# Two pieces of TensorE work change places: the last recurrence level in the first block, and a pair of transposes in the forgetting attention

## The chip, the core and the metric

One core of a Trainium2 chip runs the whole program. The metric is the device time of one execution in microseconds; the time before is the median of three runs. The engines have names in the profile: PE is TensorE's products, PEld its weight loads, DVE VectorE, ACT ScalarE, POOL GpSimd, and SP the queue that issues most of the loads.

## The reference, cut to what matters

A sequence of 256 tokens of width 1024 passes through four mixers. The first block has two layers, each with a gated recurrence (HGRN2) beside sparse attention; the second has an LRU layer and a layer with spatial gating beside forgetting attention, each with a feed-forward network. All of it is float32. The parts that the change touches:

```python
# first block, both layers: the recurrence and its gates
o_hg = hgrn2_chunkwise(heads(hq, HG_HEADS), log_f, k_hg, heads(hi, HG_HEADS))
o_hg = rmsnorm(o_hg, hgrn_onorm_g[i]).transpose(0, 2, 1, 3).reshape(B, T, HG_W)
y_hg = o_hg * jax.nn.sigmoid(hgo) * jax.nn.silu(hz)
...
kc = rmsnorm(compress(heads(kcm, KVH), cmp_pe[i, 0], cmp_w1[i, 0], cmp_w2[i, 0]), nsa_knorm_g[i, 0])
...
# second block, second layer: forgetting attention
logits = (jnp.einsum('bhqd,bhkd->bhqk', qb, k).astype(jnp.float32) * scale
          + cb[..., None] - c[:, :, None, :])
logits = jnp.where(key_pos[None, :] <= q_pos[:, None], logits, -jnp.inf)
p = jax.nn.softmax(logits, axis=-1)
return jnp.einsum('bhqk,bhkd->bhqd', p.astype(v.dtype), v)
```

## The kernel before, in words

**Products in three passes.** Every large product is written as three float32r products of rounded parts (`product3`, L477 to L481: low weight by high input, high by low, high by high). So each weight panel of 128 by 2048 is split before use: ScalarE casts the raw panel to the high part (`high_part`, L1374, the row L1381), VectorE subtracts to get the low part (`low_part`, L2006, the row L2009). There are three slots each for the raw panel, the high part and the low part. A cast waits until the panel three earlier in the row has been used up; the product waits for the low part (`split`, L465).

**An order written out by hand.** Each engine runs its own list of instructions, in order. TensorE's list is written first, and where it has issued a piece of work it notes a step with `todo(...)` in an agenda, with a place number that says how many accumulations were closed by then. ScalarE's and VectorE's lists walk this agenda and emit their share of every step in the same order; after a step they may also emit panel casts (`split_high`, L1385) and low parts (`split_low`, L2014) that the place number allows. So where a step stands in the agenda decides what stands ahead of it on two other engines.

**PSUM.** There are eight banks. `begin(name, b)` (L424) makes TensorE wait until whatever last filled bank b has been read out; `done` (L433) tells the readers that it is full. `drained` makes an engine wait for the read-out.

**The first block, around the change (both layers, L803 to L861).** The recurrence is built in eight levels, 0 to 7, each in two groups g. A level's products go to bank 7 for g = 0 and to bank 0 for g = 1 (L769); VectorE copies them out and then updates query and key (`level`, L2243), which frees the bank with the copy and lets the next level's products start with the last update (L2284, waited for in L768). `some(2)` issues one level. The gate panels hgo, hz and nz are cut into chunks of 24 products (`gate_chunk`, L787), two for each panel. The first panel, hgo0, goes to bank 6, every later one to bank 0 (L793); ScalarE copies hgo0 out in the step `copy`. Before the change the order on TensorE is: the product for the compressed hidden layer (L842), the first chunk of hgo0, level 7, the steps `k_norm` and `q_norm`, the second chunk of hgo0, the two products kc and vc (L855 and L856), the first chunk of hgo1, and so on. On VectorE the steps come as hidden (L2339), level 7, then k_norm, which begins with the low part of the panel hz0 (L2327).

**The forgetting attention (L1191 to L1214).** `tokens` (L543) multiplies by the value panels fv0 and fv1: for each half of the rows (h = 0, 1) it runs both token tiles (n = 0 into bank 0, n = 1 into bank 1). Between the two halves stands `first_value_half` (L1183), which ends in `turned(0)`: six transposes of probabilities (`turn`, L689) into banks 6 and 7. Before the change `turned(1)` follows when both tiles of the second half are done. Then come the first products of the output (L1163, into bank 0), `weigh(0)` and `weigh(1)` (probabilities by values, L709 and L711), `turned(2)`, more output products and `turned(3)`. `turned(u)` waits for the probabilities that the step `normalise u` on VectorE makes (L2047); this in turn needs the exponentials that ScalarE emits with the step `turned u-2` (L1794 to L1797). ScalarE's step `fv` (L1807) copies the two value tiles out of banks 0 and 1, and the step `fo 0` on VectorE (L2625) copies the first weighted values out.

Of the kernel before, what the change touches and what calls it, by code (L numbers as in the profile page):

```python
# [14 lines left out]
HALF = 512  # L15
# [140 lines left out]
LOADS, LOAD_NO, SPLIT_NO = panel_plan()  # L156
# [7 lines left out]
def build(nc, a, out):  # L164
# [4 lines left out]
    with ExitStack() as ctx:  # L169
# [156 lines left out]
        for name, rows in VEC_ROWS:  # L326
# [5 lines left out]
            while done_rows < rows:  # L332
                at = VEC_AT[name] + done_rows
                n = min(rows - done_rows, P - at % P)
# [86 lines left out]
        def _(pe):  # L421
            last_done = [None]

            def begin(name, b):  # L424

                k = bank_fills[b]
                bank_fills[b] += 1
                fills[name] = (b, k)
                if k > 0:
                    pe.wait_ge(psum_free[b], k)  # L430
                return ps[b]

            def done(name, ins):  # L433

                order_of[name] = len(order_of)
                ins.then_inc(psum_full[fills[name][0]], 1)
                last_done[0] = name
# [102 lines left out]
                    else:  # L540
                        ins.then_inc(psum_full[b[i]], 1)

            def tokens(names, b, keys, cols=HALF, between=None, normed=False):  # L543

                for n in range(NT):
                    begin(names[n], b + n)
                for h, key in enumerate(keys):
                    split(key)
                    if normed:
                        pe.wait_ge(xn_ready, NKH * (h + 1))  # L550
                    for n in range(NT):
                        ins = by_token(ps[b + n][:, 0:cols], parts(key, NKH, cols), n, h)
                        if h == 1:
                            done(names[n], ins)
                    if h == 0:
                        ins.then_inc(half_done, 1)
                        halves[0] += 1
                        freed(key, (half_done, halves[0]), len(order_of) - 1)
                        if between:
                            between()  # L560
                release(keys[1])
# [34 lines left out]
            for h in range(2):  # L596
                pe.wait_ge(x_landed[h], 16)
                for g in (2 * h, 2 * h + 1):
                    b = (0, 3, 4, 7)[g]
                    begin(f"x{g}", b)  # L600
                    for j in range(4):
                        c, n = 2 * g + j // 2, j % 2
# [136 lines left out]
            for l in range(DEPTH):  # L739
                todo = noting(l)  # L740
# [46 lines left out]
                def gate_chunk():  # L787

                    if not gate_chunks:
                        return  # L790
                    name, g, j = gate_chunks.pop(0)
                    key = (f"{name}{g}", l)
                    b = 6 if key[0] == "hgo0" else 0  # L793
                    if j == 0:
                        begin(f"{name}{g}_{l}", b)
                        split(key)
                    ins = chunk(ps[b][:, j * T:(j + 1) * T], parts(key), j * P)
                    if j == 1:
                        done(f"{name}{g}_{l}", ins)
                        release(key)  # L800
                        todo(("copy", f"{name}{g}"))
# [3 lines left out]
                def some(k):  # L805
                    for _ in range(min(k, len(levels))):
                        level(*levels.pop(0))
# [36 lines left out]
                done(f"hid_{l}", ins)  # L844
                todo(("hidden",))
                gate_chunk()
                some(2)
                todo(("k_norm",))
                todo(("q_norm",))


                gate_chunk()
                pe.wait_ge(w2_landed, 48 * (l + 1))
                pe.wait_ge(hidden_ready, l + 1)
                product(f"kc_{l}", 5, 32, W2[:, 0:P], HID[:, 0:32])  # L855
# [105 lines left out]
                def turned(u):  # L961
                    turn(f"n{l}", u, pidx + u)
                    todo(("turned", u))
# [67 lines left out]
                for g in range(4):  # L1031
                    b = (7, 6, 1, 2)[g]
# [14 lines left out]
            for l in range(DEPTH):  # L1047
                L = DEPTH + l
                todo = noting(L)
# [22 lines left out]
                else:  # L1072
# [119 lines left out]

                    pair_scores(0)
                    todo(("normalise", 0))
                    tokens(["fv0", "fv1"], 0, [("fv0", L), ("fv1", L)], between=first_value_half)
                    todo(("fv",))
                    turned(1)
                    todo(("normalise", 2))
                    output_rows(0, range(0, 4))
                    weigh(0)  # L1200
                    weigh(1)
# [155 lines left out]
        def _(act):  # L1357
# [27 lines left out]
            def split_high(place, most=len(SPLIT_KEYS)):  # L1385

                while next_high[0] < most:
                    q = next_high[0]
                    key = SPLIT_KEYS[q]
                    if q >= SLOTS and split_from.get(q, 1 << 30) > place or len(key) == 3 and \  # L1390
                            key not in (("gate", key[1], 0), ("value", key[1], 0)):
                        break
                    n = LOAD_NO[key]
                    high_part(n, q % SLOTS, panel_size(n), panel_free[SPLIT_KEYS[q - SLOTS]] if q >= SLOTS else None)
                    high_from[q] = place
                    next_high[0] += 1
# [102 lines left out]
            tile, r, n, c0, c1, src = gain_dma  # L1499
            act.dma_start(vrows[r:r + n, tile, c0:c1], src).then_inc(gain_rows_landed, 16)  # L1500
            turned = {}
# [27 lines left out]
            for g in range((NVT + 3) // 4):  # L1529
                s, n = 16 if g == 0 else 0, min(512, NVEC - 512 * g)  # L1530
# [172 lines left out]
            for l in range(DEPTH):  # L1703
# [61 lines left out]
                else:  # L1765
# [23 lines left out]
                    for place, step, *arg in agenda[DEPTH + l]:  # L1789
                        if step == "scores":  # L1790
                            if arg[0] == 0:
                                for k in range(2):
                                    exps_of_kind("f", 0, k, 8)
                        elif step == "turned":  # L1794
                            turned_copies("f", arg[0], pidx + arg[0])
                            if arg[0] < 2:
                                exps_of_kind("f", 1, arg[0], 8 + 1)  # L1797
                        elif step == "sg1":
                            mixed_high(DEPTH + l, None, (0, 1))
                        elif step == "zg":  # L1800
                            for n in range(NT):
                                full(act, f"zg{n}")
                                f(QN[:, n * 512:(n + 1) * 512], bank(f"zg{n}")[:, :],
                                  ACT.Gelu_apprx_tanh).then_inc(free(f"zg{n}"), 1)
                            drained(act, "zg1")
                            f(NZ[:, :], QN[:, :], ACT.Square).then_inc(act_part, 1)
                        elif step == "fv":  # L1807
                            copy_out("fv0", vh[:, 0, :], bank("fv0")[:, :])
                            copy_out("fv1", vh[:, 1, :], bank("fv1")[:, :])
                        elif step == "fo":  # L1810
                            mixed_high(DEPTH + l, ["fo0", "fo1"], (2 + arg[0],))
                        elif step == "zg_norm":
                            log_exp()
                            act.wait_ge(dve_part, 4)
                            link(f(NT16[:, :], NT16[:, :], ACT.Ln, bias=EPSC[:, 0:1], scale=1.0 / 64))
                            f(NT16[:, :], NT16[:, :], ACT.Exp, scale=-0.5).then_inc(act_part, 1)
                        elif step == "zu":
                            g = arg[0]
                            full(act, f"zu{g}")
                            f(SG[:, g * 512:(g + 1) * 512], bank(f"zu{g}")[:, :],  # L1820
                              ACT.Gelu_apprx_tanh).then_inc(free(f"zu{g}"), 1)
                        split_high(place)


                def output_drained(g):
# [115 lines left out]
        def _(dve):  # L1941
# [72 lines left out]
            def split_low(place, most=len(SPLIT_KEYS)):  # L2014

                while next_low[0] < most and next_low[0] in high_from and high_from[next_low[0]] <= place:
                    q = next_low[0]
                    n = LOAD_NO[SPLIT_KEYS[q]]
                    low_part(n, q % SLOTS, q + 1, panel_size(n))
                    next_low[0] += 1  # L2020
# [202 lines left out]
            for l in range(DEPTH):  # L2223
# [66 lines left out]
                for place, kind, *arg in agenda[l]:  # L2290
# [33 lines left out]
                                                  const(tab).unsqueeze(1).to_broadcast([P, 4, T]), ALU.mult)  # L2324
                        ins.then_inc(rope_ready, 1)
                    elif kind == "k_norm":
                        split_low(place, SPLIT_NO[("hz0", l)] + 1)  # L2327
                        dve.wait_ge(k_rinv_ready, l + 1)
                        for j in range(2):
                            s = slice(j * T, (j + 1) * T)  # L2330
# [8 lines left out]
                    elif kind == "hidden":  # L2339
# [8 lines left out]
                        V.tensor_copy(HIDV[:, :].rearrange("p (g r c) -> p g r c", g=2, r=4),  # L2348
                                      HID[:, 32:64].rearrange("p (g c) -> p g c", g=2).unsqueeze(2)
                                      .to_broadcast([P, 2, 4, 16])).then_inc(hidden_ready, 1)  # L2350
                    elif kind == "cmp_kv":
                        full(dve, f"vc_{l}")
                        V.tensor_tensor(v3(VCB, 8), const("head16").unsqueeze(2).to_broadcast([P, 8, 64]),
# [106 lines left out]
            for l in range(DEPTH):  # L2460
# [77 lines left out]
                else:  # L2538
# [4 lines left out]
                    for name in ("fq0", "fq1", "fk0", "fk1"):  # L2543
# [3 lines left out]
                        if name == "fq1":  # L2547
                            n = LOAD_NO[("ff", DEPTH + l)]
# [29 lines left out]
                    in_first = False  # L2578
                    for place, kind, *arg in agenda[DEPTH + l]:
# [50 lines left out]
                            mixed_low(DEPTH + l, 2 + g)  # L2630
                        if (kind, *arg) != ("turned", 0):
                            in_first = (kind, *arg) == ("zu", 1) or in_first and (kind, *arg) != ("scores", 1)
                        if not in_first:
                            split_low(place)
                nidx += 1
                if l == 0:
# [113 lines left out]
            for n in range(NT):  # L2750
                b = fills[f"res{n}0"][0]
# [159 lines left out]
```

## Time and profile before

| what | us |
|---|---|
| median of three runs | 976.4 (976.29 to 976.43) |
| the profiled execution, its own time | 976.13 |
| its span from first to last instruction | 974.1 |
| TensorE's products busy | 956.4 (98% of the span) |
| TensorE's weight loads busy | 876.3 (90%) |
| VectorE busy | 753.9 (77%) |
| ScalarE busy | 615.9 (63%) |
| mean granted TensorE clock | 0.999 of full speed |

The 2.0 us between the span and the profiled execution's time lie around the program. Spans of products overlap, since they are pipelined, so the distance between the starts of two products is what one costs. A row of the timeline gives start, duration, engine, line, operation, out<-in, the sizes and the count; idle time of the engine ahead of it stands in brackets with what ended it.

### The profile page before, as it was taken

The numbers are of one execution on the slowest core, as the hardware profiler recorded it, in microseconds if no ns is written. First come the engines' busy times: TensorE is split into PE (matmuls) and PEld (weight loads), VectorE is DVE, ScalarE is ACT, GpSimd is POOL, SyncE is SP. The second block draws the span as 40 slices with busy tenths as digits, with TensorE's granted clock in tenths as the row PEclk, the third lists the DMA queues.
The fourth block names the chain that finished last, engine by engine and source line by source line (L and its number), as shares of the span: only waits on it lengthen the run. The fifth ranks groups of instructions, "written<-read, shape, count | busy, mean of one in ns | idle before, by whom it ended". The sixth has DMA issues, their size and how long they took to land.

```text
span 974.1 us, 18775 instructions
## 1 busy us (share of the span) xinstructions
PE 956.4 (98%) x7618; PEld 876.3 (90%) x7618; DVE 753.9 (77%) x1132; ACT 615.9 (63%) x914; POOL 19.7 (2%) x33
## 2 busy tenths in 40 slices
PE   7999999999999999999999999999999999999997
PEld 6998989998989889999999999999898988888886
DVE  7967876787578767898788877778777598777685
ACT  5745885676447856787477556567657567555554
POOL 2000200000002000000000000000000000000000
PEclk9999999999999999999999999999999999999999
DMA  9666422465664233745546655557283446555541
GB/s 307 194 177 218 139 88 87 154 194 189 167 217 138 74 101 124 233 156 190 174 132 214 217 176 203 181 177 221 89 265 109 134 143 218 198 189 173 190 154 44
DMA packets 143870, 164.33 MB, mean 169 GB/s; under 512 B 6687, under 2 KB 130217, under 8 KB 143801
## 3 DMA queue, kind: packets, MB, share of 16 engines
q1 hardware_dynamic: 142408, 161.90, 51.5%
q0 software_dynamic: 928, 0.52, 0.4%
q8 instruction: 51, 0.84, 0.4%
q10 hardware_dynamic: 464, 0.93, 0.2%
q14 instruction: 19, 0.15, 0.0%
HBM read 161.89 MB, written 1.05 MB: 167 GB/s over the span
## 4 chain that ended last, share of the span: by engine, by line
PE 86%; DVE 7%; ACT 3%; issue 2%; DMA 1%; SPq 0%; DVEq 0%; ACTq 0%
PE ps L479 18%; PE ps L480 18%; PE ps L481 18%; PE ps L1247 14%; PE ps L1245 7%; DVE panels_low L2009 2%; ACT panels_high L1381 2%; DVE squares L1972 1%; PE ps L497 1%; PE ps L684 1%; DVE input_parts L1968 1%; DMA panels<-in_w_in 1%; PE ps L780 1%; PE ps L709 1%; PE ps L1287 1%
## 5 line engine op out<-in xcount | busy, mean ns | idle before, releaser
L2009 DVE TENSOR_TENSOR panels_low<-panels,panels_high 128x2048 fp32r<-128x2048 f32 (+1 forms) x145 | 327.5, 2261 | 67.4 <-ACT panels_high L1381 67.2
L1381 ACT CAST panels_high<-panels 128x2048 fp32r<-128x2048 f32 (+1 forms) x145 | 273.4, 1887 | 83.7 <-PE ps L481 62.2
L479 PE MATMUL ps<-input_parts,panels_low 128*128 128x256 f32 x832 | 241.5, 290 | 1.5 <-DVE panels_low L2009 0.8
L480 PE MATMUL ps<-input_parts,panels_high 128*128 128x256 f32 x832 | 235.2, 283 | 0.0
L481 PE MATMUL ps<-input_parts,panels_high 128*128 128x256 f32 x832 | 235.1, 283 | 0.0
L1247 PE MATMUL ps<-input_parts,panels_high 128*128 128x512 f32 x608 | 213.7, 395 | 0.0
L1245 PE MATMUL ps<-input_parts,panels_low 128*128 128x256 f32 x608 | 170.6, 281 | 0.7 <-DVE panels_low L2009 0.7
L479 PEld LDWEIGHTS ps<-input_parts,panels_low 128*128 128x128 f32 x832 | 159.0, 191 | 6.1 <-issue 2.6
L480 PEld LDWEIGHTS ps<-input_parts,panels_high 128*128 128x128 f32 x832 | 159.2, 191 | 0.6 <-issue 0.5
L481 PEld LDWEIGHTS ps<-input_parts,panels_high 128*128 128x128 f32 x832 | 159.2, 191 | 0.0
L1247 PEld LDWEIGHTS ps<-input_parts,panels_high 128*128 128x128 f32 x608 | 114.1, 188 | 26.1
L1245 PEld LDWEIGHTS ps<-input_parts,panels_low 128*128 128x128 f32 x608 | 114.7, 189 | 2.5 <-issue 1.3
L479 PE MATMUL ps<-ffn_hidden_high,panels_low 128*128 128x256 f32 x320 | 91.4, 286 | 0.2 <-DVE panels_low L2009 0.2
L481 PE MATMUL ps<-ffn_hidden_high,panels_high 128*128 128x256 f32 x320 | 90.7, 283 | 0.0
L480 PE MATMUL ps<-ffn_hidden_low,panels_high 128*128 128x256 f32 x288 | 81.2, 282 | 0.0
L479 PEld LDWEIGHTS ps<-ffn_hidden_high,panels_low 128*128 128x128 f32 x320 | 61.0, 191 | 1.1 <-DVE panels_low L2009 0.4
L481 PEld LDWEIGHTS ps<-ffn_hidden_high,panels_high 128*128 128x128 f32 x320 | 60.4, 189 | 0.0
L480 PEld LDWEIGHTS ps<-ffn_hidden_low,panels_high 128*128 128x128 f32 x288 | 54.3, 188 | 0.3
L1906 ACT CAST ffn_hidden_high<-values_hg 128x512 fp32r<-128x512 f32 x22 | 13.7, 621 | 57.1 <-DVE values_hg L2686 53.7
L1875 ACT COPY forget_key<-ps 128x512 f32<-128x512 f32 x36 | 21.0, 583 | 44.2 <-PE ps L1247 44.2
L479 PE MATMUL ps<-unscaled,panels_low 128*128 128x256 f32 x160 | 46.2, 289 | 0.0
L481 PE MATMUL ps<-unscaled,panels_high 128*128 128x256 f32 x160 | 45.2, 283 | 0.0
(342 smaller groups left out, 1626.7 us busy)
## 6 DMA issues: line engine op xcount, KB each, us to landing
panels<-in_ffn_up SPq DMA_DIRECT2D x44, 1024.0 KB, 5.1
panels<-in_w_in SPq DMA_DIRECT2D x29, 1024.0 KB, 5.8
panels<-in_ffn_down SPq DMA_DIRECT2D x22, 1024.0 KB, 4.9
panels<-in_mix_w_in SPq DMA_DIRECT2D x20, 1024.0 KB, 5.5
panels<-in_w_out SPq DMA_DIRECT2D x8, 1024.0 KB, 5.2
panels<-in_w_pg SPq DMA_DIRECT2D x8, 1024.0 KB, 5.0
panels<-in_mix_w_out SPq DMA_DIRECT2D x8, 1024.0 KB, 5.2
panels<-in_w_in SPq DMA_DIRECT2D x6, 512.0 KB, 5.7
```

The source lines that it names most:

```text
L479: pe.matmul(dst, w[1], x[0], start=start, stop=False if not kw else True, **kw)
L480: pe.matmul(dst, w[0], x[1], start=False, stop=False if not kw else True, **kw)
L481: return pe.matmul(dst, w[0], x[0], start=False, stop=stop, **kw)
L497: ins = pe.matmul(dst, w3[:, k, col:col + m], x3[:, k, :], start=(k == 0), stop=(k == nk - 1))
L684: ins = pe.matmul(ps[b + r][:, 0:2 * w].rearrange("p (k s) -> p k s", k=2), q[h, n * P:(n + 1) * P], keys[h, :, r, 0:w], start=False, stop ...
L709: pe.matmul(o[64 * r:64 * r + 64, :], vals(0, r), pt_lo[bb][:, r, :], start=start, stop=True, skip_group_check=True)
L1245: pe.matmul(both[:, 0, :], w_low, xh3[:, k, :], start=(k == 0), stop=True, skip_group_check=True)
L1247: ins = pe.matmul(both, w_high, x_parts[:, :, k, :], start=False, stop=True, skip_group_check=True)
L1381: nc.scalar.copy(high_slots[slot][:, 0:size], raw[n % SLOTS][:, 0:size]).then_inc(high_ready, 1)
L1875: nc.scalar.copy(sums[par][:, s, :], up_halves[half][:, :, 0, :]).then_inc(half_out, 1)
L1906: nc.scalar.copy(gh3[par], hidden[par]).then_inc(gh_ready, 1)
L2009: V.tensor_tensor(low_slots[slot][:, 0:size], raw[n % SLOTS][:, 0:size], high_slots[slot][:, 0:size].bitcast(F32), ALU.subtract).then_inc( ...
```

## The change

Three places move, and no arithmetic changes. In the first block the second chunk of hgo0 goes ahead of level 7, so that the products of level 7 stand behind two gate chunks in place of one; the steps k_norm and q_norm stay behind level 7. With this, VectorE's low part of hz0 moves from the head of the step k_norm to the end of the step hidden, which is ahead of level 7. In the forgetting attention `turned(1)` and the step `normalise 2` move from behind the second value half to a place between its two token tiles, and no panel is split at the step `turned 1`.

```diff
-            def tokens(names, b, keys, cols=HALF, between=None, normed=False):
+            def tokens(names, b, keys, cols=HALF, between=None, normed=False, amid=None):
...
                         if h == 1:
                             done(names[n], ins)
+                            if n == 0 and amid:
+                                amid()
...
                 todo(("hidden",))
                 gate_chunk()
+                gate_chunk()
                 some(2)
                 todo(("k_norm",))
                 todo(("q_norm",))
-
-
-                gate_chunk()
                 pe.wait_ge(w2_landed, 48 * (l + 1))
...
                     todo(("normalise", 0))
-                    tokens(["fv0", "fv1"], 0, [("fv0", L), ("fv1", L)], between=first_value_half)
+                    def second_value_half():
+
+                        turned(1)
+                        todo(("normalise", 2))
+
+                    tokens(["fv0", "fv1"], 0, [("fv0", L), ("fv1", L)], between=first_value_half,
+                           amid=second_value_half)
                     todo(("fv",))
-                    turned(1)
-                    todo(("normalise", 2))
                     output_rows(0, range(0, 4))
...
-                        split_high(place)
+                        if (step, *arg) != ("turned", 1):
+                            split_high(place)
...
                     elif kind == "k_norm":
-                        split_low(place, SPLIT_NO[("hz0", l)] + 1)
                         dve.wait_ge(k_rinv_ready, l + 1)
...
                                       .to_broadcast([P, 2, 4, 16])).then_inc(hidden_ready, 1)
+                        split_low(place, SPLIT_NO[("hz0", l)] + 1)
                     elif kind == "cmp_kv":
...
-                        if not in_first:
+                        if not in_first and (kind, *arg) != ("turned", 1):
                             split_low(place)
```

## Rows read from the trace of the kernel before

**Rows 1.** The page: busy time of each engine, share of the span, instructions.

```profile
PE 956.4 (98%) x7618; PEld 876.3 (90%) x7618; DVE 753.9 (77%) x1132; ACT 615.9 (63%) x914; POOL 19.7 (2%) x33
```

**Rows 2.** What TensorE waited for: total us, times, longest us.

```profile
PE ps L780 <- DVE forget_key L2284: 1.5, 2, 0.8
PE ps L695 <- DVE probs L2063: 1.1, 1, 1.1
```

**Rows 3.** Timeline of TensorE, first layer: level 7, chunk, kc, hgo1's first product.

```profile
91.08 0.68 PE L780 MATMUL ps<-query,forget_key 128*64 128x64 f32 x8
92.47 0.68 PE L780 MATMUL ps<-query,forget_key 128*64 128x64 f32 x8 [0.71 <-DVE forget_key L2284]
93.08 0.38 PE L479 MATMUL ps<-input_parts,panels_low 128*128 128x256 f32 x1
...
96.06 0.31 PE L589 MATMUL ps<-cmp_hidden,cmp_w 128*128 128x32 f32 x2
...
96.42 0.36 PE L479 MATMUL ps<-input_parts,panels_low 128*128 128x256 f32 x1
```

**Rows 4.** Timeline of VectorE, first layer: level 7's two copies, hz0's low part.

```profile
93.54 0.41 DVE L2264 COPY decay_diag<-ps 64x256 f32<-64x256 f32 x1
...
94.54 0.41 DVE L2264 COPY decay_diag<-ps 64x256 f32<-64x256 f32 x1
...
95.55 2.28 DVE L2009 TENSOR_TENSOR panels_low<-panels,panels_high 128x2048 fp32r<-128x2048 f32 x1
```

**Rows 5.** Timeline of ScalarE, first layer: hz0's cast, the end of the norms.

```profile
88.36 1.90 ACT L1381 CAST panels_high<-panels 128x2048 fp32r<-128x2048 f32 x1
...
92.69 1.06 ACT L1367 ACTIVATE gate_z<-gate_z 128x1024 f32<-128x1024 f32 x1
```

**Rows 6.** Timeline elsewhere: a low part, and the first product that waited for it.

```profile
225.60 2.29 DVE L2009 TENSOR_TENSOR panels_low<-panels,panels_high 128x2048 fp32r<-128x2048 f32 x1 [0.19 <-ACT panels_high L1381]
...
228.04 0.35 PE L479 MATMUL ps<-input_parts,panels_low 128*128 128x256 f32 x1 [0.28 <-DVE panels_low L2009]
```

**Rows 7.** Timeline of TensorE, forgetting attention: tile 1, turned(1), output, turned(2), turned(3).

```profile
746.22 0.39 PE L479 MATMUL ps<-panels_high,input_parts 128*128 128x512 f32 x1
...
748.95 0.27 PE L695 MATMUL ps<-consts,probs 128*128 128x128 f32 x1
...
749.52 0.36 PE L479 MATMUL ps<-ffn_hidden_high,panels_low 128*128 128x256 f32 x1
...
755.27 0.33 PE L695 MATMUL ps<-consts,probs 128*128 128x128 f32 x1 [1.13 <-DVE probs L2063]
...
758.85 0.27 PE L695 MATMUL ps<-consts,probs 128*128 128x128 f32 x1
```

**Rows 8.** Timeline of ScalarE in the same stretch.

```profile
745.29 0.47 ACT L1367 ACTIVATE probs<-ps,neg_max 128x256 f32<-128x256 f32 x1 [0.36 <-DVE neg_max L2043]
...
746.89 0.60 ACT L1372 COPY values_hg<-ps 128x512 f32<-128x512 f32 x1
...
751.43 0.86 ACT L1372 COPY probs_t<-ps 128x512 f32<-128x512 f32 x2
752.17 0.50 ACT L1367 ACTIVATE probs<-ps,neg_max 128x256 f32<-128x256 f32 x1
```

**Rows 9.** Timeline of VectorE in the same stretch.

```profile
746.38 4.49 DVE L2009 TENSOR_TENSOR panels_low<-panels,panels_high 128x2048 fp32r<-128x2048 f32 x2
751.57 2.29 DVE L2009 TENSOR_TENSOR panels_low<-panels,panels_high 128x2048 fp32r<-128x2048 f32 x1 [0.71 <-ACT panels_high L1381]
753.78 0.16 DVE L2056 TENSOR_SCALAR prob_sums<-prob_sums 128x4 f32<-128x4 f32 x1
...
755.13 0.68 DVE L2628 COPY squares<-ps 128x512 f32<-128x512 f32 x1
...
757.52 1.03 DVE L2063 TENSOR_TENSOR probs<-probs,prob_sums 128x256 f32<-128x256 f32 x2
```

**Rows 10.** A stretch: us, busy PE, PEld, DVE, ACT, POOL, then PEclk, DMA.

```profile
755.30:760.00 4.70, 4.70 (x41) 4.70 (x42) 2.49 (x6) 1.89 (x5) 0.00 (x0) 1.00 0.88 281
```

## The prediction

> **What bounds the kernel now.** I read the page's busy times first, then the list of TensorE's waits, then the timelines around the places that the change touches. TensorE's products are busy for 98% of the span, VectorE 77% [rows 1]. So an edit is worth only what it does to TensorE's few gaps. The list of waits names two that lie at these places: 1.5 us in two waits, one for each layer of the first block, where the products of level 7 (L780) wait for level 6's last update (L2284), and one of 1.1 us, where turned(2) (L695) waits for its probabilities (L2063) [rows 2]. Nothing else on the list lies there, and TensorE's later waits come at the end of chains that its own products start, so time won or lost here goes through to the end.
>
> **Level 7 behind the second chunk: the wait that goes.** Level 7's two groups start at 91.08 and 92.47, and the next chunk at 93.08 [rows 3]. The second group ran without a stop and took 0.61 to the next product, so both need 1.22 of the 2.00 that they took: 0.78 us were lost. Behind a second chunk, 2.98 us long (93.08 to 96.06), level 6 has been done for long, and this loss goes. hgo1's first product, at 96.42 before, would be wanted at 95.64.
>
> **What is late next.** That product opens bank 0, and bank 0 was last filled by the second group of level 7. So it waits until VectorE has copied that group out. Before, VectorE did this at 94.54, long before the bank was wanted [rows 4]. In the new order the low part of hz0 stands ahead of level 7 on VectorE. Its cast has ended at 90.26 [rows 5], so nothing holds it back: it starts at 93.54, where level 7's first copy started before [rows 4]. From the start of a low part to the next instruction go 2.21 us (751.57 to 753.78) [rows 9], so level 7's first copy comes at 95.75, the second 1.00 later, as before, and it ends 0.41 after that, at 97.16 [rows 4]. From the end of such a release to TensorE's first product go 0.15 us (227.89 to 228.04) [rows 6]. hgo1 starts at 97.31, not at 95.64: a new stop of 1.67 us takes the place of 0.78, and the layer loses 97.31 - 96.42 = 0.89 us. Two layers with the same pattern (waits of 0.7 and 0.8 [rows 2]): **+1.78 us**.
>
> The bounds for a layer are -0.78, where bank 0 would not hold TensorE at all, and +0.89, where it holds as worked out. I take the upper, as each step of it is an order in the program with a duration from a row. VectorE's sum of work is the same, so it reaches k_norm when it did.
>
> On ScalarE hgo0's copy now stands ahead of both norms and waits for the second chunk, which ends near 94.06 (95.64 less 0.36 for kc and vc, less 1.22). The copy takes 0.60 (the like copy of [rows 8]), and the norms 3.5 (90.26 to 93.75 [rows 5]), so they are out at about 98.2, well behind the 93.75 of before. VectorE takes up k_norm at 97.75 as before (its work is the same, in another order) and q_norm after that; k's inverse comes ahead of q's on ScalarE, so both are met, and POOL's additions, which follow these two steps, start when they did. The next thing that TensorE wants from ScalarE, the squares of kc, it wants behind hgo1's chunk, at 97.31 + 2.98 = 100.29. Some 2 us of cover: I price it at nothing. Without the stop at bank 0 TensorE would be there at 98.62 and this cover would be about gone. No load is issued by a moved step on any queue. The slot of hz0's raw panel comes free 2 us sooner, which only helps.
>
> A rule speaks for a smaller loss. [Rows 6] show 0.15 us between a release and the first product. The Trainium skill, TensorE: Matmul & The Clock Gate, section "Architectural detail: the array is 16× 32×32, not 1× 128×128", says that TensorE's queue can pull weight loads ahead of products in flight; if that hid the load behind each of the three new stops, the sum would be, as an estimate by that page, 0.45 us smaller. The row differs, and I keep it.
>
> **turned(1) between the tiles.** Tile 1 of the second half takes 2.73 us (746.22 to 748.95), the six transposes 0.57 (to 749.52) [rows 7]. They change places, so the output's first product is still wanted at 749.52. The gain lies at turned(2). Before, normalise 2 stood on VectorE behind the low part of a panel whose cast came late: 751.57, then 753.78 [rows 9]. Now the step comes ahead of that panel: the two low parts before it end at 750.87, normalise 2 takes 1.35 (753.78 to 755.13) [rows 9], and its result is there at 752.2. The wait of 1.13 goes.
>
> But the output's first product opens bank 0, which holds value tile 0, and ScalarE's copy of that tile now comes behind the copies and the exponentials of turned 1. ScalarE is free at 746.89, as the transposes end; the copies take 0.74 (751.43 to 752.17), the four exponentials 1.60 (745.29 to 746.89), so the tile's copy runs from 749.23 to 749.83 [rows 8]. With 0.15 [rows 6] TensorE starts at 749.98, 0.46 late. turned(2) follows 4.62 later (755.27 - 1.13 - 749.52) [rows 7], at 754.60, against 755.27: **-0.67 us**.
>
> Does turned(3) hold? It is wanted 3.58 later (755.27 to 758.85) [rows 7], at 758.18. Its probabilities come 3.42 after the start of the copy of the first weighted values (755.13 to 758.55) [rows 9], which follows the weighing, at 754.6, if VectorE is free. The late panel: tile 1's copy ends near 750.4, the cast takes 1.90 (as in [rows 5]), the low part 2.21, so VectorE is free at 754.5. Ready at 758.0 to 758.1: it just holds, with 0.1 to spare. If the stop at bank 0 were shorter, turned(3) would wait instead, so this part moves little. Bounds: -1.13, if nothing waits, and +0.64 (rival three).
>
> **The sum.** +1.78 - 0.67 = +1.11 us. The profiled execution took 976.13 and would take 977.24; the median of the runs lies 0.27 above it, and I put the same shift on it: **977.5 us**. A measurement of this kernel tells about 0.2% (1.95 us) from no change, so this is "no change", on the slow side of it.
>
> **The rivals.**
> One, faster: bank 0 does not hold TensorE in the first block. For it: the wait that is removed is plain in the list. Against it: the line that picks the bank (L793) and VectorE's 2.2 us panel. Then 2 x -0.78 - 0.67 = -2.23: 974.2. Chance 10%.
> Two: the low part of hz0 comes behind level 7 after all, since the place number does not yet allow it. TensorE starts level 7 at 94.06, its first group ends at 94.74, the second copy is out 1.41 later, at 96.15, hgo1 starts at 96.30: -0.12 for a layer, in all -0.91: 975.5. Chance 8%. This would also be the change not doing what it says.
> Three, slower: in the forgetting attention the late panel still stands ahead of normalise 2 on VectorE. It decides if ScalarE may cast that panel at an earlier step than the tiles' copies. Then its low part ends at 754.5, normalise 2 at 755.85, and turned(2) starts near 755.9, 0.64 later than before: 1.78 + 0.64 = +2.42: 978.8. Against it: the panel's slot comes free only with tile 1. Chance 8%.
> Four, slower: the granted clock falls in the new stop of 1.67 us. After the stop of 1.13 the clock was 1.00, the 2.4 GHz level [rows 10]; a stop of 1.67 within running work the trace does not have. At half the clock one chunk more of 2.98 us would be lost in each layer: some 983.5. [...] The rows show no fall. Chance 3%.
>
> **How the numbers follow.** The forecast has 66% and its own range 976.6 to 978.3, rival two 8%, and 5% is left for what I have not seen. 975.2 to 978.9 takes in the forecast, two and three, and leaves out one, four and the rest. Faster by over 0.2% (under 974.45) is rival one: 0.10. Slower by over 0.2% (over 978.35) is three, four and the forecast's edge: 0.12. Within: 0.78.
>
> **What would show it.** Right: L780 no longer in the list of TensorE's waits; in its place two waits of about 1.6 us of a product L479 for VectorE's copy L2264; one of about 0.4 for ScalarE's copy L1372; no wait at turned(2). On VectorE the low part stands ahead of L2264. Wrong: hgo1's chunk without a wait ahead of it (rival one), L2264 ahead of the low part (two), a wait of L695 for L2063 that is still there (three), PEclk under 1.00 after a stop (four).

## The result and the profile after

| what | us |
|---|---|
| before, median of 22 executions | 976.34 |
| after, median of 22 executions | 977.59 |
| ratio, 95% interval | 1.0018, 1.0012 to 1.0024 |
| the profiled execution of after, its span | 977.38, 975.3 |

The change costs 1.25 us by the medians, which is 0.13% and under the 0.2% (1.95 us) that the prediction takes as what a measurement can tell from no change; the interval of the ratio lies just clear of 1. 977.5 had been forecast. One execution of each kernel lies far off (1882.31 and 5295.99 us); the medians hardly feel it. Behind the changed places the lines of the kernel are a few higher: L780 is now L782, L695 is L697, L1372 is L1376, L2009 is L2014, L2056 is L2061, L2264 is L2269.

What TensorE waits for in the kernel after (total us, times, longest; the DMA waits are the start of the program):

```profile
PE ps L597 <- DMA q_nope<-in_norm_g: 5.6, 1, 5.6
PE ps L479 <- DVE decay_diag L2269: 3.1, 2, 1.5
PE ps L605 <- DMA forget_key<-in_x: 1.2, 1, 1.2
PE ps L479 <- DVE panels_low L2014: 0.8, 3, 0.3
PE ps L1249 <- DVE panels_low L2014: 0.8, 2, 0.4
```

Both entries of [rows 2] are gone. In the place of level 7's wait in each layer stands another, twice as long: a gate chunk's product (L479) waits until VectorE has copied level 7 out (L2269).

TensorE after, first layer: level 7, kc and vc, hgo1's first product. To be compared with [rows 3].

```profile
94.09 1.15 PE L782 MATMUL ps<-query,forget_key 128*64 128x64 f32 x16
95.17 0.41 PE L591 MATMUL ps<-cmp_hidden,cmp_w 128*128 128x32 f32 x2
95.41 0.41 PE L591 MATMUL ps<-cmp_w,cmp_hidden_rep 128*128 128x64 f32 x2
97.35 0.39 PE L479 MATMUL ps<-input_parts,panels_low 128*128 128x256 f32 x1 [1.52 <-DVE decay_diag L2269]
```

Level 7's 16 products now run in one piece, and TensorE stands still for 1.52 us behind kc and vc, ahead of hgo1. The reason is on VectorE, to be compared with [rows 4]:

```profile
93.69 2.28 DVE L2014 TENSOR_TENSOR panels_low<-panels,panels_high 128x2048 fp32r<-128x2048 f32 x1
95.89 0.41 DVE L2269 COPY decay_diag<-ps 64x256 f32<-64x256 f32 x1
...
96.89 0.41 DVE L2269 COPY decay_diag<-ps 64x256 f32<-64x256 f32 x1
```

The low part of hz0 stands ahead of the two copies; the second copy ends at 97.30 and TensorE goes on at 97.35. All that lies ahead of the changed place already comes 0.15 us later than before (hgo0's first product at 88.18, before at 88.03), so this product is 97.35 - 96.42 - 0.15 = 0.78 us late, and about as much in the second layer (a stop of 1.53).

TensorE after, forgetting attention (against [rows 7]): turned(1), tile 1, the output's first product, turned(2), turned(3).

```profile
748.00 0.27 PE L697 MATMUL ps<-consts,probs 128*128 128x128 f32 x1
...
748.57 0.48 PE L479 MATMUL ps<-panels_high,input_parts 128*128 128x512 f32 x1
...
751.68 0.38 PE L479 MATMUL ps<-ffn_hidden_high,panels_low 128*128 128x256 f32 x1
...
756.25 0.33 PE L697 MATMUL ps<-consts,probs 128*128 128x128 f32 x1
...
759.84 0.33 PE L697 MATMUL ps<-consts,probs 128*128 128x128 f32 x1
```

This stretch begins 1.77 us later than before (the second half's first product at 745.14, before at 743.37). turned(2) comes 756.25 - 755.27 = 0.98 later: 0.79 were won. The output's first product is 751.68 - 749.52 - 1.77 = 0.39 late, since its bank waits for ScalarE. The list of TensorE's waits above doesn't name this stop; the row of the product's weight load does:

```profile
751.68 0.19 PEld L479 LDWEIGHTS ps<-ffn_hidden_high,panels_low 128*128 128x128 f32 x1 [0.54 <-ACT values_hg L1376]
```

VectorE of after in the same stretch, normalise 2 and the late panel (against [rows 9]):

```profile
752.55 0.16 DVE L2061 TENSOR_SCALAR prob_sums<-prob_sums 128x4 f32<-128x4 f32 x1
...
754.03 2.29 DVE L2014 TENSOR_TENSOR panels_low<-panels,panels_high 128x2048 fp32r<-128x2048 f32 x1
```

normalise 2 (from 752.55) is now ahead of the late panel's low part (754.03), behind which it stood before. ScalarE of after, turned 1's copies and the copies of the two value tiles (against [rows 8]):

```profile
748.66 0.87 ACT L1376 COPY probs_t<-ps 128x512 f32<-128x512 f32 x2
...
750.99 1.21 ACT L1376 COPY values_hg<-ps 128x512 f32<-128x512 f32 x2
```

The value tiles come at 750.99, behind turned 1's copies and its exponentials; the first of the two copies ends near 751.6, and the output's first product starts at 751.68. By the trace the changed places sum to 2 x 0.78 - 0.79 = +0.77. The two profiled executions differ by more, by 1.25 us: 0.15 of it is there before the first changed place, 0.06 comes between the layers, and about 0.25 behind the last changed place, between 759 and 821 us, where a second profile of the same kernel (e11, below) has 0.05. In e11 the two stops are 1.59 and 1.65 us and the changed places sum to +0.96, so one profile's +0.77 is good to some 0.2. The twelve shortest executions (976.89 to 977.60, middle 977.2, all at a mean granted clock of 0.999) lie 0.85 above the median before, and 0.95 above the middle of the twelve shortest before (976.2). The rest of the median's +1.25 comes from longer executions, of which more below.

### The profile page after: what moved, and what is told of

Same layout as the page of the kernel before. It is cut to its first block, busy times and chain, and to the rows that moved or that the text cites. A ratio compares the mean times of both kernels' runs of the same rounds, so it can differ in the third digit from the quotient of the medians.

```text
span 975.3 us, 18775 instructions
## 1 busy us (share of the span) xinstructions
PE 957.3 (98%) x7618; PEld 877.0 (90%) x7618; DVE 754.1 (77%) x1132; ACT 615.9 (63%) x914; POOL 19.8 (2%) x33
## 4 chain that ended last, share of the span: by engine, by line
PE 86%; DVE 8%; ACT 3%; issue 2%; DMA 1%; SPq 0%; DVEq 0%; ACTq 0%
PE ps L479 18%; PE ps L480 18%; PE ps L481 18%; PE ps L1251 14%; PE ps L1249 7%; DVE panels_low L2014 2%; ACT panels_high L1385 2%; DVE squares L1977 1%; PE ps L497 1%; PE ps L686 1%; DVE input_parts L1973 1%; PE ps L711 1%; PE ps L782 1%; DMA forget_key<-in_x 1%; PE ps L1291 1%
## 5 line engine op out<-in xcount | busy, mean ns | idle before, releaser
L2014 DVE TENSOR_TENSOR panels_low<-panels,panels_high 128x2048 fp32r<-128x2048 f32 (+1 forms) x145 | 327.5, 2261 | 67.5 <-ACT panels_high L1385 67.4
L479 PE MATMUL ps<-input_parts,panels_low 128*128 128x256 f32 x832 | 241.3, 290 | 4.5 <-DVE decay_diag L2269 3.1
L479 PEld LDWEIGHTS ps<-input_parts,panels_low 128*128 128x128 f32 x832 | 159.2, 191 | 9.3 <-DVE decay_diag L2269 3.3
L479 PE MATMUL ps<-ffn_hidden_high,panels_low 128*128 128x256 f32 x320 | 91.7, 287 | 0.1
L479 PEld LDWEIGHTS ps<-ffn_hidden_high,panels_low 128*128 128x128 f32 x320 | 61.4, 192 | 1.0 <-ACT values_hg L1376 0.5
L479 PE MATMUL ps<-unscaled,panels_low 128*128 128x256 f32 x160 | 46.2, 289 | 0.0
```

What stands on the lines that cost most here:

```text
L479: pe.matmul(dst, w[1], x[0], start=start, stop=False if not kw else True, **kw)
L2014: V.tensor_tensor(low_slots[slot][:, 0:size], raw[n % SLOTS][:, 0:size], high_slots[slot][:, 0:size].bitcast(F32), ALU.subtract).then_inc( ...
```

## The experiments

Theory: the loss is level 7's late read-out, because VectorE does hz0's low part first; the gain is normalise 2 ahead of the late panel. Rivals: TensorE's new order costs time by itself, or what is late is ScalarE's norms (no wait of the list above names them).

**One part of the change at a time.** e1 has the first block's edit alone, e2 that of the forgetting attention alone.

e1, against the kernel before:

```diff
                 gate_chunk()
+                gate_chunk()
                 some(2)
                 todo(("k_norm",))
                 todo(("q_norm",))
-                gate_chunk()
...
                     elif kind == "k_norm":
-                        split_low(place, SPLIT_NO[("hz0", l)] + 1)
...
                                       .to_broadcast([P, 2, 4, 16])).then_inc(hidden_ready, 1)
+                        split_low(place, SPLIT_NO[("hz0", l)] + 1)
```

> The kernel before with the first block's edit alone (second gate chunk ahead of level 7, hz0's low part ahead of level 7 on VectorE); the forgetting attention as before. My theory: hgo1's first product stops for bank 0 in both layers, about 1.5 us each, while the waits of 0.71 and 0.76 at level 7 are gone; net +0.8 us a layer, so about +1.6 us against the kernel before. Its executions should also lie as wide apart as those of the whole change if these stops are what spreads them (some with a mean granted clock under 0.999). Rival: the loss of the whole change comes from the forgetting attention or from the two parts together; then this one is at -1.5 to 0 us.

e2, against the kernel before (with the conditions on `("turned", 1)` of the change):

```diff
...
-                    tokens(["fv0", "fv1"], 0, [("fv0", L), ("fv1", L)], between=first_value_half)
+                    def second_value_half():
+
+                        turned(1)
+                        todo(("normalise", 2))
+
+                    tokens(["fv0", "fv1"], 0, [("fv0", L), ("fv1", L)], between=first_value_half,
+                           amid=second_value_half)
                     todo(("fv",))
-                    turned(1)
-                    todo(("normalise", 2))
```

> The forgetting attention's edit alone; the first block as before. My theory: the wait of 1.13 us at turned(2) is gone, the output's first product starts some 0.4 us later for bank 0, net -0.8 us. Executions as close together as those of the kernel before. Rival: this part costs time too (0 to +0.6 us), or is worth the whole 1.13 us.

e2 took 975.57 against 976.33, ratio 0.9991 (0.9982 to 1.0): -0.76, as the trace of the whole had it (0.79), though the interval reaches 1. e1's two shortest executions took 977.84 and 977.85, +1.5, which is the theory's loss (2 x 0.78); its median was 979.25, ratio 1.0031 (1.0019 to 1.0044), since four executions took 979.2 to 981.0 with a mean granted clock of 0.995 to 0.997. TensorE's waits in the profiled execution of e1 (977.85):

```profile
PE ps L479 <- DVE decay_diag L2262: 3.1, 2, 1.6
PE ps L695 <- DVE probs L2061: 1.1, 1, 1.1
```

The parts are independent: the first block's stop is there without the second edit, and the wait at turned(2) is there without it too. 1.52 less 0.76 is 0.76; the trace of the whole has 0.77.

**The low part back behind level 7** (e3), and, the other way round, **the low part alone moved** (e5: the kernel before with VectorE's move and nothing else).

e3, against the kernel after:

```diff
                     elif kind == "k_norm":
+                        split_low(place, SPLIT_NO[("hz0", l)] + 1)
...
                                       .to_broadcast([P, 2, 4, 16])).then_inc(hidden_ready, 1)
-                        split_low(place, SPLIT_NO[("hz0", l)] + 1)
```

> The whole change, but hz0's low part back at the head of the step k_norm, behind level 7 on VectorE. My theory: the place of this low part is the whole of the loss. VectorE copies level 7's first group when its products end, about 94.8, the second group is out at about 96.2, and hgo1's first product starts near 96.35 instead of 97.35: 1.0 us a layer better than the whole change, -0.2 a layer against the kernel before, so with -0.8 from the forgetting attention about -1.1 us in all. A stop for bank 0 of about 0.5 us stays in each layer. Rival: the second chunk ahead of level 7 is what costs, wherever the low part stands: +0.5 to +1.2 us as for the whole change.

e5, against the kernel before:

```diff
                     elif kind == "k_norm":
-                        split_low(place, SPLIT_NO[("hz0", l)] + 1)
...
                                       .to_broadcast([P, 2, 4, 16])).then_inc(hidden_ready, 1)
+                        split_low(place, SPLIT_NO[("hz0", l)] + 1)
```

> The kernel before with one edit alone: hz0's low part ahead of level 7 on VectorE. TensorE's order is as before, so the wait of 0.7 us at level 7 stays. My theory: bank 0 is freed at 97.2 as in the whole change, so hgo1's first product, wanted at 96.45, stops for about 0.8 us: +0.8 to +0.9 us a layer, +1.7 us in all, as much as the first part's edit costs in its fastest executions (977.84 against 976.33). The two stops of 0.7 and 0.8 us stand apart. If the executions of the first part lie wide apart (977.84 to 980.97, mean granted clock down to 0.995) because one stop of 1.5 us makes the clock fall in some of them, these here lie close together, near 978.0. Rival: whatever holds TensorE up in this stretch spreads them, and these do too; or the low part's move alone costs little (under +0.6 us), and the second chunk ahead of level 7 is needed for the loss.

e3 took 975.00, 0.9986 (0.9977 to 0.9995): -1.33 where the change has +1.25, so putting one VectorE instruction back turns the sign. TensorE's stop in the first layer of e3, by the timeline:

```profile
96.45 0.38 PE L479 MATMUL ps<-input_parts,panels_low 128*128 128x256 f32 x1 [0.46 <-DVE decay_diag L2269]
```

e5 took 978.01 against 976.41, 1.0017 (1.0008 to 1.0026): +1.60, the same loss as e1's with TensorE's order of before. Level 7's wait stays, and a second stop joins it, as TensorE's timeline of e5 shows:

```profile
93.05 0.68 PE L780 MATMUL ps<-query,forget_key 128*64 128x64 f32 x8 [0.72 <-DVE forget_key L2284]
...
97.80 0.39 PE L479 MATMUL ps<-input_parts,panels_low 128*128 128x256 f32 x1 [0.60 <-DVE decay_diag L2264]
```

So the whole loss of the first block is VectorE's move, and TensorE's new order by itself is a gain. The rival of a costly order is out. The 0.46 us left in e3 say that even with the low part behind, level 7's two copies are late for a bank that is wanted right behind kc and vc.

**Another bank for hgo1** (e4, against the kernel after), so that it needs no read-out of level 7.

```diff
-                    b = 6 if key[0] == "hgo0" else 0
+                    b = {"hgo0": 6, "hgo1": 4}.get(key[0], 0)
```

> The whole change, but hgo1's chunks go to bank 4 in place of bank 0. Bank 4's last content, the sums of the key squares, is read by ScalarE's first norm at about 95.4. My theory: bank 0 is what holds TensorE, so the stop of 1.5 us goes and hgo1 starts at about 95.75; the squares of kc are then wanted at 98.7, just when ScalarE has them (98.6), so at most 0.1 us is lost there. 1.5 us a layer better than the whole change: about -2.3 us against the kernel before. Rival: TensorE stops elsewhere for the same late VectorE work (at kc's squares or at the cross product, which waits for level 7's update), and less than half of this comes back: -0.8 us or worse.

It took 974.94, 0.9984 (0.9975 to 0.9994): -1.39, and 0.9 less was gained than expected. The stop at hgo1 is gone, as the theory has it. But the time did not all go through. TensorE's timeline of e4, further on in the first layer:

```profile
103.13 0.46 PE L883 MATMUL ps<-decay_diag,values_hg 128*128 128x128 f32 x2 [0.18 <-issue]
```

The recurrence's output products come some 0.35 us late in each layer. With TensorE 1.7 us ahead (hgo1 at 95.66), ScalarE is what is late: its cast of hz1 (98.55, 1.89 us) stands ahead of the copies that these products read. The squares of kc, which stand behind the norms on ScalarE, are late too, by less: they start 3.04 us behind hgo1's first product (98.70 - 95.66), before it was 2.96 (99.38 - 96.42), and the cross product follows them after 0.24 in place of 0.14, in all 0.18 us.

**That cast behind the step `cross`** (e6: e4 and this).

```diff
-                    if not parts_out and (not in_units or step == "turned" and arg[0] % 2 == 1):
+                    if step not in ("cmp_kv", "kc_norm", "spread") and not parts_out and (
+                            not in_units or step == "turned" and arg[0] % 2 == 1):
```

> The whole change with hgo1 in bank 4 (the run before, -1.39 us), and on ScalarE the cast of hz1 moved from the step cmp_kv to the step cross, behind the copies of the decay blocks and of the cross product. In the bank 4 run the recurrence's output products start at 103.13, 0.35 us after the chunk ahead of them allows, and ScalarE works without a gap from 94 on with that cast in the middle. My theory: ScalarE is late with those copies by this cast of 1.9 us; moved, the products start at once, 0.35 us a layer: -2.0 to -2.1 us against the kernel before. Rival: what is late there is VectorE or the products themselves, and nothing comes back (-1.4), or the later cast holds up VectorE's low part of hz1 and its chunk (worse than -1.4).

974.02, 0.9977 (0.9968 to 0.9986): -2.39. The wait at L883 is gone. That is 1.0 us better than e4, where two layers of 0.35 had been expected; the traces show the two waits gone and the 0.18 at kc's squares still there, so some 0.3 of the 1.0 is not accounted for.

**And the 0.39 us at the output's bank** (e7: e6, with value tile 0 copied ahead of turned 1's exponentials on ScalarE, and the low part of the output's third panel behind normalise 3 on VectorE).

```diff
+                            if arg[0] == 1:
+                                copy_out("fv0", vh[:, 0, :], bank("fv0")[:, :])
...
-                            copy_out("fv0", vh[:, 0, :], bank("fv0")[:, :])
...
-                        if not in_first and (kind, *arg) != ("turned", 1):
+                        if not in_first and (kind, *arg) not in (("turned", 1), ("fv",), ("fo", 0), ("turned", 2)):
```

> As the run before (hgo1 in bank 4, hz1's cast later), and in the forgetting attention ScalarE copies value tile 0 ahead of the exponentials of turned 1 instead of behind them, with VectorE's low part of the output's third panel behind normalise 3 in place of ahead of the copy of the first weighted values. My theory: the output's first product then starts at once instead of 0.24 us late, and normalise 3, no longer behind that low part, keeps up: 0.2 to 0.3 us better than the run before, about -2.3 us against the kernel before. Rival: turned(3) waits for normalise 3 instead and takes the gain back (0 to -0.1 us against the run before).

973.74, 0.9973 (0.9963 to 0.9984): -2.67, the lowest median of all, 0.28 below e6, whose executions (973.65 to 974.68) overlap with these (973.54 to 974.09). TensorE's list of waits now holds the start and five short ones elsewhere:

```profile
PE ps L597 <- DMA q_nope<-in_norm_g: 6.4, 1, 6.4
PE ps L479 <- DVE panels_low L2016: 0.8, 3, 0.3
PE ps L1249 <- DVE panels_low L2016: 0.7, 2, 0.4
PE ps L605 <- DMA forget_key<-in_x: 0.5, 1, 0.5
```

**The suspected cost doubled** (e8: the whole change, and hz0's low part computed twice in a row; the second result equals the first).

```diff
...
+                        step(V.tensor_tensor(low_slots[s][:, :], raw[n % SLOTS][:, :], high_slots[s][:, :].bitcast(F32),
+                                             ALU.subtract))
+                        settle()
                         split_low(place, SPLIT_NO[("hz0", l)] + 1)
```

> The whole change with hz0's low part computed twice in a row on VectorE, ahead of level 7 (the same values written twice). It doubles the suspected cost. My theory: the stop ahead of hgo1 grows by one low part, from 1.53 to about 3.75 us a layer, so +4.4 us on the whole change: 981.6 us if the clock keeps its level. If a TensorE that stands still there has its granted clock lowered, the profile shows PEclk 0.5 in the stretch behind the stop, and each 1 us at half the clock loses about 0.5 us: then 983 to 988 us. Rival: VectorE's time at this place is not what holds TensorE, and the time rises by much less than 4 us.

It took 985.85, 1.0098 (1.0083 to 1.0114). The stop grew by the low part's length, from 1.52 to 3.86 us, by TensorE's timeline of e8:

```profile
99.88 0.58 PE L479 MATMUL ps<-input_parts,panels_low 128*128 128x256 f32 x1 [3.86 <-DVE decay_diag L2269]
```

That makes 977.38 + 2 x 2.34 = 982.1 of its profiled 984.69. The other 2.6 us are the clock: behind the stops TensorE falls another 1.36 us back against the kernel before in the first layer and 1.21 in the second. Stretches of 2 us of e8 (us; busy PE, PEld, DVE, ACT, POOL; granted clock, DMA share, GB/s):

```profile
96.00:98.00 2.00, 0.03 (x1) 0.00 (x0) 1.97 (x2) 1.97 (x4) 0.00 (x0) 1.00 0.01 4
98.00:100.00 2.00, 0.12 (x1) 0.12 (x1) 2.00 (x6) 1.97 (x4) 0.00 (x0) 0.88 0.19 36
100.00:102.00 2.00, 2.00 (x10) 2.00 (x11) 1.97 (x6) 0.60 (x1) 0.00 (x0) 0.50 1.04 347
102.00:104.00 2.00, 2.00 (x15) 2.00 (x15) 1.97 (x4) 0.00 (x0) 1.09 (x3) 0.76 0.43 150
104.00:106.00 2.00, 2.00 (x19) 2.00 (x19) 2.00 (x2) 1.41 (x5) 2.00 (x3) 1.00 0.20 21
...
302.00:304.00 2.00, 2.00 (x12) 2.00 (x11) 1.97 (x5) 0.00 (x0) 0.00 (x0) 0.50 1.06 370
```

TensorE was idle from 96 on; behind the stop it works at 0.50, the 1.2 GHz level, and gets through 10 products in 2 us, where it does 19 from 104 on, at 1.00.

**Where the long executions of e1 and of the change lose their time.** Three more profiles on this question: e9 and e10 are e1 unchanged, e11 is the whole change, unchanged.

> The first block's edit alone, profiled once more, since four of its six executions were 1.4 to 3.1 us longer than the fastest and the one profiled was a fast one. Theory (the granted clock falls in or behind the stop of 1.5 us): if this profiled execution takes 979.0 or more, the two-microsecond stretches show a granted clock under 1.00 between 96 and 101 us, or between 294 and 299 us, or both, and nowhere else before 970 us; the two stops are 1.5 us as before, and behind each fall the layer loses 1 to 2 us. If it takes 977.8 to 978.2, every stretch up to 970 us shows 1.00. Rival (the longer executions lose their time elsewhere, in a load or an engine that is late): the clock is 1.00 in both stretches of an execution of 979.0 or more, and the list of TensorE's waits holds another wait, or a longer one, by the difference.

> The same kernel a third time, with the same two expectations: over 979.0 with a granted clock under 1.00 behind a stop of the first block (theory), or over 979.0 with the clock at 1.00 there and another wait longer (rival); 977.8 to 978.2 with 1.00 throughout tells neither.

> The whole change, profiled once more. In 9 of its 21 undisturbed executions it took over 978. Theory: if the profiled execution is one of these, a stretch behind a stop of the first block shows a granted clock under 1.00, and the forgetting attention's second half, which has a stop of 0.3 us only, shows 1.00. Rival: 1.00 in all of these and another wait longer. At 977.0 to 977.6 every stretch up to 970 us is at 1.00.

They took 978.47, 977.89 and 977.58, so none is a long one, and every stretch of 2 us up to 970 us shows 1.00 in all three. In e9 the stops are the same (1.52 and 1.52); 0.5 of its 0.6 us over e1 are already there at hgo1 (97.95 against 97.43), so, the stops being as long, they come from ahead of the stop. This told neither theory from rival.

## Why the prediction was right

**The first block** went as predicted in kind. Level 7's wait went, and bank 0 became the next thing late, behind hz0's low part on VectorE; e3, e4 and e5 show each link by itself. Predicted was a loss of 0.89 us a layer, measured 0.78. VectorE was met to the hundredth: level 7's second copy, predicted to end at 97.16, and 0.15 later by the later start, ended at 97.30. What was mis-sized is the 0.15 us from the release to the first product, taken from [rows 6]: here it is 97.35 - 97.30 = 0.05. The Trainium skill's rule that was weighed there (TensorE: Matmul & The Clock Gate, "Architectural detail: the array is 16× 32×32, not 1× 128×128": weight loads can be pulled ahead) would have taken all 0.15 away at this stop; 0.10 of it went, but not in that way, as the row of this product's weight load shows:

```profile
97.35 0.19 PEld L479 LDWEIGHTS ps<-input_parts,panels_low 128*128 128x128 f32 x1 [1.66 <-DVE decay_diag L2269]
```

The load too starts only behind the release, 0.05 us after it, as it does at the output's bank (751.68). So no weight load was pulled ahead of these waits. Why the release takes 0.05 us here and 0.15 in [rows 6] stays open.

**The forgetting attention** gained 0.79, predicted 0.67. normalise 2 went ahead of the late panel, and the output's first product waited for ScalarE: 0.39 us, predicted 0.46. e2 showed the gain alone; e7, with two edits at once, gave back some 0.28. turned(3) just held, as worked out: its probabilities were done at 759.78, and it started at 759.84.

**ScalarE's late norms** were priced at nothing, and within this change they cost nothing: no wait for them is on the list. The remark that this cover would be about gone without the stop at bank 0 was right: in e4 kc's squares start at 98.70, where 98.62 had been worked out, and that costs 0.18 us a layer. What the prediction did not see is the larger part, the copies behind hz1's cast: 0.35 us a layer.

**The sum** was +1.11, the changed places in the trace have +0.77, and the median +1.25. That 977.5 lies so near to 977.59 is partly luck, in errors that offset: each of the three stops came out about 0.1 us better than predicted, and against that some executions were longer, for a reason that stays open (rival four, held at 3%, is the candidate). The nearness of the profiled execution (977.38, forecast 977.24) rests on some 0.45 us that differ between the two profiles away from the changed places.

**The rivals.** One (bank 0 doesn't hold), two (the low part comes behind level 7) and three (the late panel still ahead of normalise 2) are refuted by the timelines of VectorE and TensorE above. Four, the granted clock that falls in the new stop, is not seen in any profile of a 1.5 us stop (five were taken, of the change, e1, e9, e10 and e11), and the full price of 2.98 us a layer was never paid; e8 paid about 1.3. But some means speak for it: 0.995 to 0.997 in e1's four long executions and in five of the change's nine over 978, 1.2 to 3.3 us longer than the shortest of their kernel. In e8's profile one stretch of 0.50 behind each of two stops cost 1.3 us each and took the mean to 0.995, from 0.999 in the change's profile; so one such stretch would explain a mean of 0.997 and two 0.995, with about the times measured. Against it, three long executions of the change have means of 0.998 or 0.999 (978.32 to 978.65), and one of 982.82 has 0.945, far lower than its time accounts for. That the clock was lost behind the stops is argued from e8 and not shown.

## What to carry to other kernels

Behind a wait that is removed, look at the next buffer that the freed engine fills: who reads it out, and what stands ahead of that read-out in the reader's order. Here one VectorE instruction of 2.2 us, put ahead of two copies of 0.4, turned a gain of 1.3 us into a loss of 1.25. Where the order of the reader can't be changed, another bank can do the same (e4: -1.39), and the next engine that is late then shows (here ScalarE's cast, moved in e6).

## What the runs showed of the hardware that had not been expected

In e8 a stop cost more than its length, since the clock fell. A stop of 3.86 us there was followed by a granted clock of 0.50 in both layers of the first block, some 1.3 us a layer on top. The Trainium skill, TensorE: Matmul & The Clock Gate, section "HAM oscillation — how this bites in real kernels", says that a TensorE left idle is throttled back and starts cold; e8's rows agree. Behind the stops of 1.52 to 1.65 us in five profiles the granted clock stayed at 1.00.

With about the same loss divided in two the executions lay closer together: e5, with stops of 0.72 and 0.60 us, took 977.76 to 978.53 in eleven executions at a mean clock of 0.998 to 0.999, while e1, with one stop of 1.5, took 977.84 to 980.97 in six, at 0.995 to 0.998. Where the clock falls in e1's longer executions stays open, since none of them was profiled.
